# A decoder layer on one core: w_o multiplied in fp32, weights of two experts loaded earlier, expert rows in halves of the array and one expert behind

## What is computed

```python
z = x @ w_in + b_in                                # 1024 -> 5376
# attention branch A (12 heads) and convolution branch C, then
branch_c = silu(layer_norm(conv)) @ w_conv_out + b_conv_out
branch_a = attn @ w_attn_out
y = (g_a * branch_a + g_c * branch_c) @ w_o        # 1024 -> 1024
h = layer_norm(ALPHA * x + y)
# router: best of 4 groups, then the best 2 of its 8 experts; 32 experts of 1024 -> 512 -> 1024
moe = sum over the 2 chosen e of gate_e * ((silu(h @ w_eg[e]) * (h @ w_eu[e])) @ w_ed[e])
out = layer_norm(ALPHA * h + moe)
```

## Time and profile before

| | us |
|---|---|
| median of 3 runs | 1112.72 |
| lowest and highest | 1110.96, 1114.45 |
| the profiled execution | 1111.08 |
| its span in the profile | 1109.3 |
| granted TensorE clock, mean | 0.965 |
| TensorE busy (matmuls) | 1021.5 (92%) |
| VectorE busy | 624.5 (56%) |
| ScalarE busy | 286.8 (26%) |
| GpSimd busy | 217.2 (20%) |
| bytes moved | 293.55 MB |

### The profile page before, as it was taken

The page is one execution under the profiler, slowest core; times in us unless marked ns, Lnnn a source line. Parts: engine busy times, 40 slices in busy tenths (PEclk is TensorE's granted clock), DMA queues, the critical chain, the costliest instruction groups (busy, mean ns, idle before and its releaser), DMA issues. The chain is left out here.

```text
span 1109.3 us, 30843 instructions
## 1 busy us (share of the span) xinstructions
PE 1021.5 (92%) x12960; PEld 792.5 (71%) x12960; DVE 624.5 (56%) x1386; ACT 286.8 (26%) x600; POOL 217.2 (20%) x193
## 2 busy tenths in 40 slices
PE   9999999999999899995999999999899998989880
PEld 8999998899997678874566665656565655656650
DVE  2699999810126728477367655445445453535435
ACT  3322321232225662011122222122121212212123
POOL 2453440232210014002111112111111212110100
PEclk9999999999998999996899999999999999999995
DMA  8467834136423521326999999999999999999624
GB/s 293 166 252 269 313 116 162 67 138 219 151 86 139 204 82 64 127 81 245 390 372 409 402 418 403 403 403 380 395 358 401 380 357 378 345 376 348 259 74 164
DMA packets 45696, 293.55 MB, mean 265 GB/s; under 512 B 11519, under 2 KB 15231, under 8 KB 26173
## 3 DMA queue, kind: packets, MB, share of 16 engines
q1 hardware_dynamic: 22285, 163.96, 38.3%
q10 hardware_dynamic: 12624, 102.63, 22.8%
q0 software_dynamic: 10720, 25.98, 7.9%
HBM read 286.83 MB, written 41.12 MB: 296 GB/s over the span
## 5 line engine op out<-in xcount | busy, mean ns | idle before, releaser
L978 PE MATMUL ps<-region_b,scratch 128*32 128x256 f32 x2976 | 174.7, 389 | 24.3 <-DMA region_b<-in_gate_up_rows 24.3
L978 PE MATMUL ps<-region_a,scratch 128*32 128x256 f32 x3168 | 180.3, 381 | 10.5 <-DMA region_a<-in_gate_up_rows 10.5
L995 PE MATMUL ps<-z_conv_gates,x_columns 128*32 128x256 f32 x3072 | 172.1, 379 | 0.0
L1718 DVE STREAM_TRANSPOSE scratch<-x_columns 32x256 f32<-32x256 f32 x384 | 165.8, 432 | 9.7 <-DMA x_columns<-h_rows,token_rows 3.6
L978 PEld LDWEIGHTS ps<-region_b,scratch 128*32 128x32 f32 x2976 | 107.5, 112 | 85.5 <-issue 26.3
L978 PEld LDWEIGHTS ps<-region_a,scratch 128*32 128x32 f32 x3168 | 113.8, 111 | 71.0 <-issue 15.8
L995 PEld LDWEIGHTS ps<-z_conv_gates,x_columns 128*32 128x32 f32 x3072 | 110.4, 110 | 55.3
L1375 DVE SCALAR_TENSOR_TENSOR z_conv_gates<-scratch,column_vectors,z_conv_gates 128x512 f32<-128x512 f32 x240 | 143.0, 673 | 0.0
L1724 DVE SCALAR_TENSOR_TENSOR x_columns<-ps,column_vectors,x_columns 128x128 f32<-128x128 f32 x96 | 33.7, 351 | 166.8 <-ACT x_columns L1272 165.0
L1272 ACT ACTIVATE x_columns<-ps 128x128 f32<-128x128 f32 x96 | 26.6, 277 | 377.6 <-PE ps L978 377.6
L579 PE MATMUL ps<-z_split,region_b_split 128*128 128x272 f32 x384 | 111.2, 290 | 0.0
(11 more groups left out here) (266 smaller groups left out, 1337.9 us busy)
## 6 DMA issues: line engine op xcount, KB each, us to landing
region_b<-in_gate_up_rows SPq DMA_DIRECT2D x21, 2048.0 KB
region_a<-in_gate_up_rows ACTq DMA_DIRECT2D x21, 2048.0 KB, 42.2
z_conv_gates<-in_down_rows SPq DMA_DIRECT2D x32, 1024.0 KB
z_conv_gates<-in_down_rows ACTq DMA_DIRECT2D x32, 1024.0 KB
region_a<-in_gate_up_rows SPq DMA_DIRECT2D x12, 2048.0 KB
region_b<-in_w_in_pairs SPq DMA_DIRECT2D x20, 1024.0 KB, 5.0
region_b<-in_gate_up_rows ACTq DMA_DIRECT2D x10, 2048.0 KB
region_b<-in_cache_tiles POOLq DMA_DIRECT2D x16, 768.0 KB, 4.9
```

The source lines that it names most:

```text
L978: last = pe.matmul(ps[j * R:(j + 1) * R, r, 0:2 * QF], ecols[s][:, r, 4 * c + k, :], w[:, k, j, :], start=c + k == 0, stop=c + k == 4)
L995: last = pe.matmul(ps[j * R:(j + 1) * R, RB + r, 0:QD], hcols[:, r, k * R:(k + 1) * R], w[:, k, j, :], start=k == 0, stop=k == KF - 1)
L1718: last = ve.transpose(ecols[s][q * R:(q + 1) * R, r, :, :].rearrange("p k c -> p (k c)"), xg[s][r * R:(r + 1) * R, q * QD:(q + 1) * QD])
```

## The change

- **w_o.** The split is gone: `rows_out` does one float32 matmul per k and half, with the weights as they are loaded. GpSimd writes the merged column tile to gc[m]. The small tile becomes tile 1, right behind tile 0, and is multiplied in four column groups side by side (`small_out`); tiles 0 and 2 are done together first. TensorE waits for all 8 `br_used` rather than 7. Tile 4, now a whole one, is normalised in one part and after the routing of tile 3.
- **Early loads.** gates(0) second half and both of gates(1) are issued at `merged` 6, down(0) and down(1) at `merged` 8; gates(2) and down(2) still wait for the first gather.
- **Halves.** The first 64 of the 96 rows of a block are multiplied in two halves of the array's columns (128x512 each), the remaining 32 in four groups as before. Gate weights are brought for 64 rows in two copies and 32 rows in four.
- **One behind.** TensorE's order becomes gates(e), down(e-1), `turn_hidden(e)`: three transposes of the hidden rows on TensorE, which VectorE copies out (`hidden_copy`). down(e+2) is loaded when down(e-1) has been multiplied. GpSimd's scatters are one expert further behind its gathers.
- The layouts of the weights in memory follow; their sizes don't change.

```diff
-TILES = [(t * P, min(P, N - t * P)) for t in range((N + P - 1) // P)]
+SMALL = 1
+TILES = [(r * P, P) for r in range(SEQ // P)]
+TILES.insert(SMALL, (SEQ, NS))
...
                 if t == 1:
-                    sp_e.wait_ge(x_split, XQ + 6)
+                    sp_e.wait_ge(merged, 6)
                     load_gates(0, 0, 1)
-            sp_e.wait_ge(y_ps, NTT + 1)
-            for s in range(2):
-                sp_e.wait_ge(krow_stored[s], 16 * 3)
-            load_gates(1, 1, 0)
+                    load_gates(1, 1, 0)
+                    sp_e.wait_ge(merged, KD)
+                    for s in range(2):
+                        sp_e.wait_ge(krow_stored[s], 16 * 3)
+                    load_down(0, 0)
+                    load_down(1, 1)
+            sp_e.wait_ge(y_ps, NTT)
             sp_e.wait_ge(gathered[0], 16)
-            load_down(0, 0)
             load_gates(2, 2, 0)
-            load_down(1, 1)
             load_down(2, 2)
 
             def following(e, s):
-                sp_e.wait_ge(gu_ps, RB * e + RB)
+                sp_e.wait_ge(rest_ps, e + 1)
                 load_gates(e + 3, s, 0)
-                sp_e.wait_ge(dn_ps, RB * e + RB)
-                load_down(e + 3, s)
+                sp_e.wait_ge(dn_big_ps, e)
+                load_down(e + 2, (s + 2) % SLOTS)
...
-                        pe.matmul(out, ga_hi[k][:, c0:c0 + n], wo_hi[:, k, cols], start=k == 0, stop=False)
-                        pe.matmul(out, ga_hi[k][:, c0:c0 + n], wo_lo[:, k, cols], start=False, stop=False)
-                        last = pe.matmul(out, ga_lo[k][:, c0:c0 + n], wo_hi[:, k, cols], start=False, stop=k == KD - 1)
+                        last = pe.matmul(out, gc[k][:, c0:c0 + n], wo[:, k, cols], start=k == 0, stop=k == KD - 1)
+            def small_out():
+                c0, n = TILES[SMALL]
+                for k in range(KD):
+                    for j in range(GROUPS):
+                        last = pe.matmul(ps[j * R:(j + 1) * R, 6, 0:QD], gc[k][:, c0:c0 + n], wo[:, k, j * QD:(j + 1) * QD],
+                                         start=k == 0, stop=k == KD - 1)
...
-            for r in range(RB):
+            for k, (first, rows, times) in enumerate(((0, BIG, 2), (BIG, REST, GROUPS))):
                 for i in range(NK):
                     n = TILES[i % NTT][1]
-                    for j in range(GROUPS):
...
+            def gate_up_big(e, s, weights, ready):
+                pe.wait_ge(xgt_sb, RB * e + RB - 1)
+                if not (isinstance(e, int) and e == 0):
+                    pe.wait_ge(big_hid, e)
+                for c in range(2):
+                    ready(c)
+                    w = weights[c].rearrange("p (k h n) -> p k h n", k=4, h=2)
+                    for k in range(4):
+                        for half in range(2):
+                            last = pe.matmul(ps[half * BIG:(half + 1) * BIG, 2, :], ecols_big[s][:, 4 * c + k, :], w[:, k, half, :],
+                                             start=c + k == 0, stop=c + k == 4)
+                last.then_inc(big_ps, 1)
+            def turn_hidden(e):
+                pe.wait_ge(big_hid, e + 1)
+                for c in range(2):
+                    pe.transpose(hid_ps[:, c * P:(c + 1) * P], hid_big[:, c * P:(c + 1) * P], eye)
+                pe.wait_ge(rest_hid, e + 1)
+                pe.transpose(hid_ps[:, 2 * P:3 * P], hid_rest, eye).then_inc(hid_turned, 1)
...
             def expert(e, s, rounds):
-                gate_up(e, s, gu_place[s], lambda c: pe.wait_ge(gu_loaded[s][c], 16 * rounds))
-                down(e, dn_place[s], lambda: pe.wait_ge(dn_loaded[s], 32 * rounds))
+                before_s = (s + 2) % SLOTS
+                gates_of(e, s, rounds)
+                rows_of(e - 1, before_s, rounds - (s == 0))
+                turn_hidden(e)
```

More of the change, by code:

```diff
@@ new lines, in gate_up_rest @@
+            def gate_up_rest(e, s, weights):
+                pe.wait_ge(xgt_sb, RB * e + RB)
+                if not (isinstance(e, int) and e == 0):
+                    pe.wait_ge(rest_hid, e)
+                for c in range(2):
+                    w = weights[c].rearrange("p (k h two n) -> p k h two n", k=4, h=2, two=2)
+                    for k in range(4):
+                        for j in range(GROUPS):
+                            n0 = (j % 2) * P
+                            last = pe.matmul(ps[j * REST:(j + 1) * REST, 3, 0:2 * P].rearrange("p (two n) -> p two n", two=2),
+                                             ecols_rest[s][:, 4 * c + k, :], w[:, k, j // 2, :, n0:n0 + P], start=c + k == 0, stop=c + k == 4)
+                last.then_inc(rest_ps, 1)
@@ new lines, in down @@
+                for k in range(KF):
+                    for j in range(GROUPS):
+                        last = pe.matmul(ps[j * REST:(j + 1) * REST, 6, 0:256], hcols_rest[:, k, :], w[:, k, j * 256:(j + 1) * 256],
+                                         start=k == 0, stop=k == KF - 1)
+                last.then_inc(dn_rest_ps, 1)
+                if not (isinstance(e, int) and e == 0):
+                    pe.wait_ge(yo_big, e)
+                for k in range(KF):
+                    for half in range(2):
+                        last = pe.matmul(ps[half * BIG:(half + 1) * BIG, 5, :], hcols_big[:, k % 2, k // 2, :], w[:, k, half * 512:(half + 1) * 512],
+                                         start=k == 0, stop=k == KF - 1)
@@ L1010, in _ @@
             keep_running(20)
-            for e in range(LOOP.start):
-                expert(e, e, 1)
+            gates_of(0, 0, 1)
+            turn_hidden(0)
+            expert(1, 1, 1)
+            expert(2, 2, 1)
             with pe.Fori(LOOP.start // 3, LOOP.stop // 3) as i:
@@ new lines, in expert @@
+            def expert(e, s, before, load=(True, True)):
+                silu_big(e)
+                silu_rest(e)
+                if load[0]:
+                    load_gates(e + 3, s)
+                last_s = (s + 2) % SLOTS
+                rows_back(e - 1, last_s, before)
+                if load[1]:
+                    load_down(e + 2, last_s)
+            silu_big(0)
+            silu_rest(0)
+            load_gates(3, 0)
+            expert(1, 1, None)
+            expert(2, 2, None)
@@ L1300, in _ @@
+            expert(3, 0, None)
+            expert(4, 1, 1)
+            expert(5, 2, 1)
+            with ac.Fori(LOOP.start // 3 + 1, LOOP.stop // 3) as i:
+                for s in range(SLOTS):
+                    expert(3 * i + s, s, i - (s == 0))
+            expert(27, 0, 8)
+            expert(28, 1, 9)
+            expert(29, 2, 9, (False, True))
+            expert(30, 0, 9, (False, False))
+            expert(31, 1, 10, (False, False))
+            rows_back(31, 1, 10)
             ac.wait_ge(idx_set, 1)
```

406 lines of the change are left out of this document (191 added, 215 removed).

## The result

The changed kernel takes 1114.76 us (median of 20 runs, 1110.97 to 1117.95), the kernel before, run beside it, 1112.47 (1109.79 to 1116.1). The ratio is 1.002, 95% interval 1.001 to 1.0029: slower by about 2.3 us. Forecast were 1111.5 us and -1.1; the measurement lies inside the range of 1103 to 1121, but on the other side of the kernel before. The profiled execution took 1115.75 us with a span of 1113.8, 4.5 us more than the span before; where the time went is told on these two spans.

A forecast was written before the change was run, and what follows sets the result against it. Weight loads after the first gather were taken to bound the kernel. +8.2 later start, +2.7 idle queue, -17.85 three downs fewer, +6.1 tail, -0.3 gave -1.1 us: 1111.5 us, range 1103 to 1121.

The forecast's parts named there:

- What bounds the kernel: Expert loop: loads need 17.7 us an expert against TensorE's 15.5; the last landing, unevenly loaded DMA engine sets the pace.
- w_o: w_o matmuls: fp32 in four tiles costs 55.2 us as before, 3.5 us longer in all, starting 1.9 us later, ending 507.1.
- First gather: From w_o's end through norm, logits and routing: the first gather lands 8.2 us later, at 529.1 (bounds 527 to 531).
- Start of the experts: Gate weights on TensorE take 5.1 us, to 530.7; with 6.9 us of idle matmuls expert 0 begins at 537.6, not 534.4.
- The loads: Weight loads behind the first gather: three downs fewer, one expert's bytes, save 17.85 us; 29.33 experts take 523.5 us.
- The empty queue: Load queue stands still 1.1 to 3.2 us before gates 3 and 0 to 1.1 before gates 4; taken as 2.7 us.
- The tail: From gates 31 to the end of the last down: 21.9 us instead of 15.75, +6.1.
- The halves: Two column halves cost as much as four groups; transposes add 0.4 us, TensorE 15.9 us an expert, covered by the loads.
- Rival 1: Early load pace was the burst's, so 4.7 us go and the idle queue costs nothing: 1104 us, chance 0.33.
- Rival 2: TensorE becomes the bound through tiling changes, deciding from 16.9 us an expert; at 17.2 us 1121 us, chance 0.13.
- Rival 3: Routing ends later still, a missed VectorE/TensorE turn before tile 4 delays gather and loads: 1116 to 1119 us, chance 0.10.
- Rival 4: The halves run one after the other, TensorE 26 us an expert: about 1380 us, chance 0.02.

The follow-up runs named there:

- the spread rows: Kernel before with one constants line changed so filled gather and scatter rows no longer lie next to each other: 1070.19 us, 0.9611; same line in the changed kernel: 1099.35 us.
- the gap filled: Changed kernel with 20 matmuls of ones on TensorE in front of the turning of tile 4: 1113.37 us, ratio 1.001.
- the series of spread rows: Kernel before with 4.4, 3.9, 3.2 or 2.6 filled rows in the fullest group instead of 5.75: 1096.95, 1090.54, 1079.89, 1070.19 us; packed at the other end 1114.86.
- narrow matmuls: Changed kernel with the 20 matmuls without use ahead of expert 0 made 32 columns wide: 1111.21 us, ratio 0.9987.
- late downs: Changed kernel with the down weights of experts 0 and 1 loaded behind the first gather again: 1121.71 us, ratio 1.0089.

## Why the forecast missed

**What bounds the kernel: right.** The loads set the end from the first gather on. Doing more or less on TensorE (16.78 and 16.18 us an expert) moved nothing that the measurement can tell; two downs later cost 7.0 us; that the landing rate falls because some engines run dry agrees with the spread rows. The waits for loads began before expert 23 and not at about 10: by the forecast's own terms gates n land at 531.8 + 17.85 x (n - 1.67) and TensorE comes to them at 549 + 15.9 x (n - 1), so the first wait would stand before expert 16; with the measured 552 and 16.40 it is expert 23.

**w_o: right in kind.** It starts at 437.12, as forecast, and its last product ends at 505.6 (507.1 forecast). The norm of tile 4 was done at 511.6 us, where the forecast had 513.2.

**First gather: right, by two errors that cancel.** 530.04 against 529.1 in this trace, 529.2 on average of seven. The norm was done 1.6 us earlier than forecast, but what follows on TensorE was priced at the higher clock level; after the gap of 4.8 us it ran at the lower one, the turning 0.9 us longer than with the gap filled and the logits 1.8 us longer than in the earlier trace rows, and that took back the 1.6 and more. That the sum fitted so well is luck.

**Start of the experts: 1.2 us late,** 538.77 against 537.6. The gate weights on TensorE don't wait for the gather; they began at 528.06, 2.5 us later than the forecast had them (517.38 + 8.2), and they and the idle matmuls took 10.7 us rather than 12.0.

**The loads: the step that failed.** The forecast said "a down half pair is a third of an expert's bytes" and took three downs fewer at 17.85 / 3 each, 17.85 us. But 17.85 us is not a time of weight bytes alone: the series of spread rows splits it into about 15.5 us of weights and 2.3 us of gathered and scattered rows (5.75 x 0.40). The rows of all 32 experts still have to be moved; only weights go. Three downs are then worth 15.5, 2.3 us less. The forecast had named the uneven load in its first part and didn't carry it into its sum.

How well do the runs show the term itself? The changed kernel with narrow matmuls has no empty stretch and is 1.1 us below the kernel before run beside it; with +8.3 for the gather, +6.9 for the tail and -0.6 for the rest that leaves -15.7 for three downs, 1.2 us either way by the interval of its ratio. Its trace gives less: 1057.00 - 528.70 = 528.3 us against 541.3, so -13.0. Two downs alone are the difference between late downs and narrow matmuls, 10.5 us by the medians and 539.2 - 528.3 = 10.9 in the traces. That fits 10.3 (two thirds of 15.5), but the intervals don't exclude the forecast's 11.9. So the medians and the traces both have the term smaller than 17.85. That the rows make the difference is worked out from the series; no run isolates it, and up to 2.5 us between medians and traces stay open.

**The empty queue: 0.8 us short, and in another place.** It is worth 3.5 against 2.7. The forecast had 1.1 to 3.2 us ahead of gates 3 and up to 1.1 ahead of gates 4; it was 0.4 and 3.1. The forecast hadn't seen that down 3, now one behind, no longer fills the time between gates 3 and gates 4, nor the low clock in expert 1.

**The tail: 0.7 us short.** 22.6 us: 16.5 for gate/up 31, down 30 and the transposes, 0.65 of waiting for VectorE's copy of the hidden columns, 5.5 for down 31 to its end.

With the terms as measured, 9.1 - 15.5 + 3.5 + 6.9 - 0.6 = +3.4 us, or +2.6 with the average gather. The medians have +2.3, the two profiled spans +4.5.

**The halves: right that it doesn't matter, wrong in size.** 0.86 us more an expert, not 0.36: three transposes are 0.48 between the starts, gate/up costs 10.50 rather than 10.36, down 5.42 rather than 5.18.

**The rivals.** Rival 1 (free idle, an early pace of the burst) fell with the narrow matmuls and with a pace of 18.0 us in them (1057.00 - 528.70 over 29.33), where it had 17.7. Rival 2 gave the point of 16.9 us from which TensorE decides; with 16.40, and even with 16.78, it stayed short of it. The Trainium skill's rule of a drain at each change of the tiling mode ("TensorEngine Tiling (Array Packing)", key properties) has at most 0.38 us an expert to account for here (0.14 + 0.24, the excess without the transposes, if the halves otherwise cost what the groups do), and nothing on the time. Rival 3 fell: VectorE began the norm of tile 4 at 505.92, 0.4 us after the last product. Rival 4 fell: the halves do run side by side. The chances, 0.34, 0.41 and 0.25, put the side that came last; the sum stood 1.1 us from no change with terms of 18 us in it, and one of them was 13% off.

## What to carry to other kernels

A pace read off a trace is a price for exactly the mix it was read from; before it is used for a part of that mix (weights without rows), split it, if need be by a run that changes one ingredient. Where the DMA share sinks while an engine waits for loads, ask first which transfers always fill the same rows: here one line of constants took 42 us off, while the early loads, the new w_o and the halves together added 2.3. And an edit that takes instructions out ahead of a long loop can move the loop over the edge of what stays loaded; look at the instruction packets before believing the time.

## What the runs showed of the hardware

- The filled rows of 96-row gathers and scatters cost 0.40 us an expert for each row in the fullest group of 6, against an estimated 15.5 us for 6.3 MB of weights, whichever end is filled (17.85 and 17.95 us).
- 20 matmuls fewer in front of TensorE's loop (40 instructions of the trace: a matmul and a weight load each) and 63 more packets of code, 115 instead of 52 of 16 KB each, with 89 us more of time. The Trainium skill ("Runtime: NRT & Kernel Launch", "Instruction fetch mechanics") gives TensorE room for 2048 instructions in blocks of 256 and calls prefetch purely sequential; the trace agrees with the 16 KB blocks, but with the 20 matmuls the loop is not loaded again from round to round (no packet between 634 and 968 us), where that section says that no instruction cache benefits from locality.
- A gather behind weights on other queues waits for them: with 8.4 instead of 4.2 MB issued 10 to 16 us ahead of it, it landed 9.9 us after its issue instead of 4.3, and 7.0 us later in all.
- Behind 4.8 us without work on TensorE the same 16 logit matmuls took 3.62 or 3.63 in place of 1.98 us, at a granted clock of 0.50, in all of the seven traces that have the gap.
